# One-core two-layer transformer: two weight slabs of five projections split one block earlier, and the sum of two attentions moved from GpSimd to VectorE

## What is computed

```python
# first layer: two attentions, gated, summed, projected
y_a = jnp.einsum('bse,ed->bsd', o_a.reshape(b, s, MLA_HEADS * MLA_V), w_o_a)
y_b = jnp.einsum('bse,ed->bsd', o_b.reshape(b, s, DSA_HEADS * DSA_HEAD_DIM), w_o_b)
y = jax.nn.sigmoid(g_a) * y_a + jax.nn.sigmoid(g_b) * y_b
x = x + jnp.einsum('bsd,de->bse', y, w_out)
...
# second layer
gates = jax.nn.sigmoid(p[..., r_end:] + b_gate[l])
y = gates[..., :D_MODEL] * y_conv + gates[..., D_MODEL:] * y_rwkv
h = layer_norm(ALPHA * h + y @ w_o[l], ln1_g[l], ln1_b[l])
...
def conv_gated_mlp(h, ffn_up, ffn_dw, ffn_down):
    u = causal_dwconv(h @ ffn_up, ffn_dw)
    return (jax.nn.silu(u[..., D_FF:]) * u[..., :D_FF]) @ ffn_down
```

## Time and profile before

| | |
|---|---|
| median of 3 runs | 2303.87 us (2294.82 to 2307.06) |
| profiled execution, its own time | 2301.43 us |
| span of its trace | 2299.7 us |
| mean granted TensorE clock | 0.933 |
| TensorE busy | 2036.5 us, 89% |
| VectorE busy | 1290.7 us, 56% |
| ScalarE busy | 944.5 us, 41% |
| GpSimd busy | 728.1 us, 32% |

### The profile page before, as it was taken

How to read it: one execution, slowest core, us unless ns; L and a number is a source line. 1 busy time by engine, 2 the same in 40 slices (tenths; PEclk the granted TensorE clock), 3 DMA queues, 4 the chain that set the end, 5 groups by cost and what they waited for, 6 DMA issues and landing times. The chain is left out here.

```text
span 2299.7 us, 37103 instructions
## 1 busy us (share of the span) xinstructions
PE 2036.5 (89%) x14878; PEld 1719.0 (75%) x14878; DVE 1290.7 (56%) x1883; ACT 944.5 (41%) x1476; POOL 728.1 (32%) x390
## 2 busy tenths in 40 slices
PE   6999998789699999779999977588889979999797
PEld 4777835366477777579999866588669969999684
DVE  3446825432588888331899667456441157777402
ACT  4213228722578777442222354144233243332312
POOL 2432300052111112033444236331034525555341
PEclk9998998989799999889999988699889989999899
DMA  4221210022599999222323202220122312222231
GB/s 173 83 74 55 92 55 1 1 74 73 210 355 344 354 337 361 91 75 91 121 92 127 68 28 77 65 40 19 39 93 92 93 37 93 92 92 92 64 93 45
DMA packets 88339, 256.60 MB, mean 112 GB/s; under 512 B 26176, under 2 KB 27344, under 8 KB 87424
## 3 DMA queue, kind: packets, MB, share of 16 engines
q1 hardware_dynamic: 84448, 244.39, 31.3%
q0 software_dynamic: 3744, 10.11, 1.3%
HBM read 235.59 MB, written 18.87 MB: 111 GB/s over the span
## 5 line engine op out<-in xcount | busy, mean ns | idle before, releaser
L1448 DVE TENSOR_TENSOR moe_wlo<-moe_ring,moe_whi 128x1024 fp32r<-128x1024 f32 x198 | 234.8, 1220 | 55.7 <-ACT moe_whi L1444 54.1
L508 PE MATMUL acc<-h_xhi,h_whi 128*128 128x264 f32 x816 | 235.3, 288 | 18.0 <-DVE h_xlo L443 12.1
L508 PE MATMUL acc<-h_xlo,h_whi 128*128 128x264 f32 x816 | 234.0, 287 | 0.0
L508 PE MATMUL acc<-h_xhi,h_wlo 128*128 128x264 f32 x816 | 233.7, 286 | 0.0
L1444 ACT ACTIVATE moe_whi<-moe_ring 128x1024 fp32r<-128x1024 f32 x198 | 205.3, 1058 | 64.3 <-DMA moe_ring<-moe_slabs 39.5
L508 PE MATMUL acc<-ff_xhi,ff_whi 128*128 128x258 f32 x704 | 201.3, 286 | 11.7 <-DVE ff_xlo L443 11.6
L508 PE MATMUL acc<-ff_xhi,ff_wlo 128*128 128x258 f32 x704 | 200.4, 285 | 0.0
L508 PE MATMUL acc<-ff_xlo,ff_whi 128*128 128x258 f32 x704 | 200.3, 285 | 0.0
L382 POOL TENSOR_TENSOR h_wlo<-ring,h_whi 128x1024 fp32r<-128x1024 f32 x51 | 122.5, 2404 | 194.9 <-ACT h_whi L377 194.9
L508 PEld LDWEIGHTS acc<-h_xhi,h_whi 128*128 128x128 f32 x816 | 156.3, 192 | 19.7 <-POOL h_wlo L382 16.3
L1882 DVE SCALAR_TENSOR_TENSOR acc<-cp,par,acc 128x528 f32<-128x528 f32 x232 | 159.2, 765 | 0.0
(11 more groups left out here) (497 smaller groups left out, 5225.6 us busy)
## 6 DMA issues: line engine op xcount, KB each, us to landing
ring<-slabs SPq DMA_DIRECT2D x213, 512.0 KB, 3.5
moe_ring<-moe_slabs SPq DMA_DIRECT2D x198, 512.0 KB, 5.3
tok_rows<-h_tok SPq DMA_DIRECT2D x5, 512.0 KB, 2.9
h_spill<-x2r SPq DMA_DIRECT2D x1, 2112.0 KB, 7.4
v_spill<-rw_v SPq DMA_DIRECT2D x1, 2112.0 KB, 7.4
y_spill<-cp SPq DMA_DIRECT2D x8, 264.0 KB, 4.6
rw_v<-v_spill SPq DMA_DIRECT2D x1, 2112.0 KB, 8.1
x2r<-h_spill SPq DMA_DIRECT2D x1, 2112.0 KB
```

Source lines behind the costliest of these rows:

```text
L508: mm = nc.tensor.matmul(acc[j][0:rows, s, 0:t1 - t0], wp[:, at:at + rows], xp[:, t0:t1], start=(k == 0 and m == 0), stop=(k == kt - 1 and ...
L1448: tensor_tensor(wlo[u % AHEAD][:, :], ringm[u % AHEAD][:, :], whi[u % AHEAD][:, :].bitcast(F32), ALU.subtract).then_inc(w_lo[u % 2], 1)
```

## The change

In five places ScalarE and GpSimd now split the first two slabs of a projection in the block ahead of it; `Weights` objects are made one block earlier for that, and w_o's object with its two buffers also serves w_out. `Weights.act` and `Weights.pool` skip a slab that is already split. `ahead(name)` is the first two slabs of a projection. The sum of the attentions goes from GpSimd to VectorE, one addition behind each multiplication from the tenth on. The core of the diff:

```diff
             def pool(self, pool, n):
+                if self.next_low is not None and n < self.next_low:
+                    return
+                self.next_low = n + 1
                 pool.wait_ge(hi_made, split_rank[n] + 1)
...
+            def ahead(self, name):
+                return slab_range(name)[:2]
...
# normalize (before ffn_up; split=(w, "ffn_up")), both at the stream's start
+                        def _(pool):
+                            for n in split[0].ahead(split[1]):
+                                split[0].pool(pool, n)
...
                     def _(act):
+                        if split:
+                            for n in split[0].ahead(split[1]):
+                                split[0].act(act, n)
...
# attend
                         if p + 1 < NP:
                             exps(p + 1)
+                        if p == NP:
+                            for n in w.ahead("w_o_a"):
+                                w.act(act, n)
                         if p >= 1:
                             store(p - 1)
...
+                @b.gpsimd
+                def _(pool):
+                    for n in w.ahead("w_o_a"):
+                        w.pool(pool, n)
...
# block of w_o_a and w_o_b
                     w.all_act(act, ["w_o_a", "w_o_b"])
+                    for n in w.ahead("w_out"):
+                        w.act(act, n)
...
+                    def both(i):
+                        dve.wait_ge(oy_out, 9 + i)
+                        nc.vector.tensor_tensor(h[:, i, :], h[:, i, :], gb[:, i, :], ALU.add).then_inc(y_sum, 1)
...
                         nc.vector.tensor_tensor(d[:, i % 8, :], acc[i % 4][:, 0, :], g[:, i % 8, :],
                                                 ALU.mult).then_inc(oy_out, 1)
+                        if i >= 9:
+                            both(i - 9)
+                    both(7)
+                    dve.wait_ge(y_sum, 8)
...
                     w.all_pool(pool, ["w_o_a", "w_o_b"])
-                    for i in range(8):
-                        pool.wait_ge(oy_out, 9 + i)
-                        link("pool", pool, nc.gpsimd.tensor_tensor(h[:, i, :], h[:, i, :], gb[:, i, :], ALU.add))
+                    for n in w.ahead("w_out"):
+                        w.pool(pool, n)
...
# out_projection
-                w = Weights(px, "wout")
...
# group_norm_and_gate
                     nc.scalar.activation(fold(root[:, :], T3), A(2, T3, 16), ACT.Sqrt,
                                          bias=k0("eps", 1, EPS_GN)[0:16, :]).then_inc(rooted, 1)
+                    for n in w.ahead("gate_b"):
+                        w.act(act, n)
...
+                    w.pool(pool, w.ahead("gate_b")[0])
                     for i in range(8):
+                        if i == 4:
+                            w.pool(pool, w.ahead("gate_b")[1])
                         pool.wait_ge(shifted, i + 1)
...
# ffn, block of ffn_up
                         tile_loop(act, w, [("ffn_up", KD, 2 * NF)], take)
+                        for n in wd.ahead("ffn_down"):
+                            wd.act(act, n)
                         silu(act, NF - 1)
...
+                            if f == NF - 1:
+                                wd.pool(pool, wd.ahead("ffn_down")[0])
                             pool.wait_ge(silued, f + 1)
```

More of the change, by code:

```diff
@@ L356, in program, with __init__ @@
         class Weights:
-            def __init__(self, ctx, tag, depth=3, hi_at=None):
+            def __init__(self, ctx, tag, depth=3, hi_at=None, side="left"):
                 self.depth = depth
-                self.hi = [sbt(ctx, f"{tag}_whi{i}", [P, 1024], F32R) if hi_at is None else
+                own = lambda n: ctx.enter_context(nc.sbuf_tensor(f"{tag}_{n}", [P, 1024], F32R, side=side))
+                self.hi = [own(f"whi{i}") if hi_at is None else
                            nc.alloc_sbuf_tensor_at(f"{tag}_whi{i}", [P, 1024], F32R, offset=hi_at + 4096 * i) for i in range(depth)]
-                self.lo = [sbt(ctx, f"{tag}_wlo{i}", [P, 1024], F32R) for i in range(depth)]
-                self.first = None
+                self.lo = [own(f"wlo{i}") for i in range(depth)]
+                self.first = self.next_low = None
+            def ahead(self, name):
+                return slab_range(name)[:2]
             def act(self, act, n):
@@ L522, in program, with normalize @@
         norm_base = [0] * len(norm_sems)
-        def normalize(tag, src, dst, kt, t, mean, gain, bias=None, eps=EPS_RMS, func=None, sent=None, left=None, enter=None):
+        def normalize(tag, src, dst, kt, t, mean, gain, bias=None, eps=EPS_RMS, func=None, sent=None, left=None, enter=None, split=None):
             centre = bias is not None
@@ L648, in first_block @@
                     with ExitStack() as att:
-                        attention_part(att, xt, h, k1, mix_rstd, c1_here)
-                out_projection(xt, h)
+                        w_out = attention_part(att, mix, xt, h, k1, mix_rstd, c1_here)
+                    out_projection(xt, h, w_out)
                 with ExitStack() as mx:
@@ L1015, in attention_part @@
             causal = lambda qt: k1("causal", (qt + 1) * P, T1 - (qt + 1) * P)
+            w = Weights(mix, "wo", 2, side="right")
             attend([(lambda hd, lo, hi: qa[0:96, hd, lo:hi], lambda hd, n: ka[0:96, hd, 0:n], va,
@@ L1019, in attention_part @@
                      lambda hd, n: kb[64 * (hd % 2):64 * (hd % 2) + 64, hd // 2, 0:n], vb,
-                     lambda qt: sel[qt][:, :] if qt else causal(0), HD ** -0.5, ob)])
+                     lambda qt: sel[qt][:, :] if qt else causal(0), HD ** -0.5, ob)], w)
             late.close()
@@ L1059, in _, with out_projection @@
                     load_slabs(sp, "w_o_b")
-        def out_projection(xt, h):
+            return w
+        def out_projection(xt, h, w):
             xo_ready, xo_out = sem("xo_ready", True), sem("xo_out", True)
@@ L1919, in mixers @@
                 recurrence(r, k, v, kk, a, a, wc, k2, kk_r)
-                with ExitStack() as gx:
-                    group_norm_and_gate(sbt(gx, "gn_scratch", [P, KD, T1]), r, k, v, a, xg, k2, h)
-                merge(h, r, k, a)
+                with ExitStack() as mx:
+                    w = Weights(mx, "mg")
+                    with ExitStack() as gx:
+                        group_norm_and_gate(sbt(gx, "gn_scratch", [P, KD, T1]), r, k, v, a, xg, k2, h, w)
+                    merge(h, r, k, a, w)
         def conv_out_and_keys(cp, cv, cv_at, v_at, wa, r, k, kk, a, wc, k2, v):
@@ L3077, in ffn @@
                 ln1_rstd = sbt(fx, "ln1_rstd", [P, T3])
-                normalize("ln1", ht, ht, KD, T3, k0("mean1024"), None, True, EPS_LN, left=ln1_rstd)
+                wd = Weights(fx, "fd", 2, free_at)
+                wux = fx.enter_context(ExitStack())
+                w = Weights(wux, "ff")
+                normalize("ln1", ht, ht, KD, T3, k0("mean1024"), None, True, EPS_LN, left=ln1_rstd, split=(w, "ffn_up"))
                 with ExitStack() as ux, block() as b:
```

16 lines of the change are left out of this document (8 added, 8 removed).

## The result

| | before | after |
|---|---|---|
| median | 2304.02 us (2294.82 to 2309.53, 8 runs) | 2290.48 us (2281.69 to 2296.94, 8 runs) |
| ratio, 95% interval | 1 | 0.9944 (0.9929 to 0.996) |
| profiled execution, span | 2301.43, 2299.7 us | 2292.32, 2290.5 us |
| mean granted clock | 0.933 | 0.931 |

The change makes the kernel 0.56% faster, 13.5 us by the medians; 2289.4 was forecast. The same kernel run again with the last group of experiments gave 2286.58 us against 2304.0 (0.9924, 0.99 to 0.9947): the two sets of medians put the gain at 13.5 and 17.4 us.

The account below looks back on a forecast made before the run. TensorE, busy 89% of the span, was taken to bound a chain of projections, with gains at their starts: 0.8+4.1+5.1+3.4+1.1 = 14.5 us, so 2286.9 against the profiled execution, 2289.4 against the median; range 2280 to 2299.5.

Parts of the forecast that it names:

- The whole: Sum of the gains at five projection starts: 14.5 us, giving 2289.4 us against the median shown; forecast's chance 0.61.
- w_o_a, 0.8: Start of w_o_a: VectorE stalls behind GpSimd's second split, TensorE starts as now, its 1.08 us second wait goes; 0.8 us gained.
- The last addition: End of the attentions' sum: GpSimd's split goes first, VectorE's last addition ends near 513.0, w_out's block opens 0.7 us later.
- w_out, 4.1: Start of w_out: no split ahead of the operand, first matmul at 514.75 against 516.86, first tile 4.1 us earlier.
- Two buffers at w_out: Two weight buffers replace three; each slab's split, some 3.6 us, hides behind a 5.44 us tile with 1.8 us to spare.
- rival (c): w_out's two buffers make TensorE stop at each of six tiles; slower, 2318 us; chance 0.04.
- gate_b, 5.1: Start of gate_b: first matmul 1702.25 against 1705.06, 4.29 us of low clock, first tile 5.1 us earlier.
- the large end's 7.0: gate_b's gain if the clock does not fall at all in the shorter pause: 7.0 us.
- ffn_up, 3.4: Start of ffn_up: splits move into the normalization's block, TensorE is fed every 1.42 us; 3.4 us gained, range 1.9 to 3.9.
- ffn_down, 1.1: Start of ffn_down: GpSimd's split stalls the last tap, block end 2.0 us later, but no second stall; 1.1 us gained.
- Rival (b): A block's end waits for GpSimd's unfinished split, felt only at w_o_a: sum 13.3 us, 2290.6 us; chance 0.06.
- Rival (a): Small ends at all starts: long low clock, second fall at ffn_up, races lost; sum 9.2 us, 2294.7 us; chance 0.29.

## Why the prediction was right, and where not

- **The whole**: 14.5 us forecast, 14.0 by the stages, 13.5 by the medians. The forecast held; but the sum is right partly by luck, since errors cancel: the starts of w_o_a and w_out gained 1.7 us more than their terms, and the pitch took 2.3 that no term had.
- **w_o_a, 0.8**: measured 1.15, and 1.9 to 2.2 in the seven other traces of this form. The mechanism was as written: VectorE lost the race by 0.18 us (463.04 against 462.86) and stood until GpSimd's second split ended at 465.21. TensorE started 6.96 us after the last copy in place of 7.06, and its second wait went. What mis-sized the term is the clock. It was taken to return when it does now; the low stretch ended 12.7 us after the last copy before, 12.0 after, and 9.8 to 10.3 in the seven others.
- **The last addition**: this step of the prediction failed. "I let GpSimd go first" was written; VectorE's addition was not held in any trace of this form. The block opened 0.6 us after the additions, 1.5 us earlier than now, not 0.7 later. In its place GpSimd's delayed split held the first `yo_xlo` (516.39, VectorE's eight took 5.73 in place of 8 times 0.62), which the prediction let through in 0.7 us. **w_out, 4.1**: measured 5.46; with VectorE first it had been priced at 5.2. TensorE's waits ahead of w_out's second and third block, 0.41 and 1.14 us before, are gone, as said. The Trainium skill (SBUF — State Buffer, Who interferes with whom) says that whoever issues first holds the pair. At w_o_a the trace agrees, with 0.18 us between the two. Here it can't tell: the split is recorded as begun 0.01 us ahead of the addition, and yet only the split stretched, to 2.90. No run moves one against the other, so what decides so close a meeting stays open, and a forecast good to 0.2 us can't give it.
- **Two buffers at w_out**: right. No wait of TensorE between 525 and 576 us is recorded, and rival (c) falls. The wrong part is what was not asked: the new buffers' place. The sentence that failed is "TensorE runs on at the same pace (2.72 us a tile of w_o": it was 2.80, and with w_out's tiles it cost 2.3 us.
- **gate_b, 5.1**: 5.13. Start 2.77 us after the last gated tile, 4.29 of low clock assumed, 3.4 recorded. In four other traces the clock did not fall there and the stage took 8.80: 6.6 us, the large end's 7.0.
- **ffn_up, 3.4**: 3.44. Fed every 1.42 us, and no second fall of the clock.
- **ffn_down, 1.1**: 1.15, and 1.0 to 1.7 in the other traces of this form. The tap's stall (2.71, "about 2.8") and the block's 2.0 us are as written.
- **Rival (b)**, the block's end waits for GpSimd: false, by the 0.51 us at 462.38. The Trainium skill (Perfetto Trace Analysis, GPSIMD Engine Instruction) has the sequencer ready for its next instruction once one is pushed to the wait queue, and the trace agrees: the block's end passed 2.8 us before the second split was done.
- **Rival (a)**, small ends: no stage stood at its small end; each was at or above its term.

## To carry over

When buffers move, compare the matmul pitch of the projections that read them. In this kernel, at 512 columns, weights and moving operand a multiple of 256 bytes apart gave the better pitch each time. Cut traces into stages between fixed instructions: they repeat to 0.1 us where the clock does the same, where whole executions differ by ten. A split moved ahead pays only if nothing is left that holds the same start, and a start moved into a stretch of low clock can be worth little: at ffn_down 2.4 us earlier gave 0.45 us in one pair of traces and 0.8 in another.

## What the chip showed unasked

With 512 columns, weights and moving operand not a multiple of 256 bytes apart in the partition cost 0.002 to 0.007 us of 0.227 per matmul by the stages, up to 3%. gate_b's matmuls of 258 columns whose low operand lies 128 bytes off its weights keep 0.119 to 0.120 in every trace, so this is shown for 512 columns only. TensorE's clock stayed low for 13.7 us at ffn_down in thirteen of the fourteen traces, though TensorE began to work 8.8, 10.4 or 11.3 us after ffn_up's last copy; in the fourteenth it was 10.2. At gate_b it stayed full in four executions and fell for 3.4 us in five with the same pause of 2.77 us.
